# A fused two-layer decoder trunk: where a ones product stands in the DeltaNet projection, and when the output projections load their activations

## The reference, cut to what matters

```python
qkv = causal_dwconv_silu(qkv, conv_w)          # h @ w_in, a four-tap convolution per channel, SiLU
q, k, v = jnp.split(qkv, [A_QK, 2 * A_QK], axis=-1)
q = l2_norm(q.reshape(bsz, seq, A_HEADS, A_DK))  # x * rsqrt(sum(x*x over the 128 of a head) + eps)
k = l2_norm(k.reshape(bsz, seq, A_HEADS, A_DK))
...
return (o * jax.nn.silu(z)) @ w_out              # output projection of each mixer
x = x + gate * rms_norm(y, a_post_g[j])          # residual rows x are added behind it
```

## Time and profile before

| what | value |
|---|---|
| median of three runs | 3534.41 us |
| profiled execution, its own time | 3540.65 us |
| span of its records | 3539.0 us |
| PE busy | 3193.6 us (90%) |
| DVE, ACT, POOL busy | 1756.8, 1218.3, 940.8 us |
| mean granted TensorE clock | 0.949 of full speed |
| L892 square, L878 Ln, L880 Exp, one each | 1914, 1974, 1918 ns |
| L889, L878, L880 table load, one each | 1283 ns |
| L474 and L478 on POOL, mean of one | 3331 and 2586 ns |

### The profile page before, as it was taken

One profiled execution on the slowest core, in us unless ns is written; L12 is line 12 of the kernel. 1 busy time (PEld: TensorE's weight loads), 2 busy tenths in 40 slices (PEclk: granted clock), 3 DMA queues, 4 the chain that ended last, 5 costly groups with the idle time before them and its releaser, 6 DMA issues. The chain is left out here.

```text
span 3539.0 us, 41132 instructions
## 1 busy us (share of the span) xinstructions
PE 3193.6 (90%) x15158; PEld 2315.6 (65%) x15158; DVE 1756.8 (50%) x2771; ACT 1218.3 (34%) x2078; POOL 940.8 (27%) x739
## 2 busy tenths in 40 slices
PE   5889899999978997978999699996999999999798
PEld 4666566888867886866888578884444444444476
DVE  4454444566645665544211142115676777675433
ACT  4344445444414453224111131110344444444311
POOL 0578860233235440100000000001333333333210
PEclk8999899999989998988999899996999999999899
DMA  5233422567555654555431244317243433330333
GB/s 204 74 118 101 131 91 61 187 209 223 177 154 192 200 182 147 180 163 158 119 83 48 87 145 116 107 48 173 60 108 81 108 84 79 81 84 10 110 128 119
DMA packets 270102, 436.35 MB, mean 123 GB/s; under 512 B 73214, under 2 KB 170118, under 8 KB 259612
## 3 DMA queue, kind: packets, MB, share of 16 engines
q1 hardware_dynamic: 230812, 332.18, 31.8%
q0 software_dynamic: 23520, 86.21, 7.8%
q10 hardware_dynamic: 15600, 15.73, 1.5%
HBM read 283.10 MB, written 150.82 MB: 123 GB/s over the span
## 5 line engine op out<-in xcount | busy, mean ns | idle before, releaser
L2123 ACT ACTIVATE at_probs<-at_logits 128x512 f32<-128x512 f32 (+3 forms) x640 | 331.2, 532 | 414.0 <-PE at_logits L1986 381.7
L173 PE MATMUL pa_y<-pa_h_high,pa_w_high 128*128 128x512 f32 x1056 | 422.6, 400 | 7.5 <-ACT pa_acc L839 5.5
L1960 DVE TENSOR_REDUCE at_partial<-at_rough 128x1 f32<-128x512 f32 (+1 forms) x600 | 349.8, 605 | 129.1 <-PE at_rough L1948 76.3
L174 PE MATMUL pa_y<-pa_h_low,pa_w_high 128*128 128x512 f32 x1056 | 413.0, 391 | 0.0
L175 PE MATMUL pa_y<-pa_h_high,pa_w_low 128*128 128x512 f32 x1056 | 412.7, 391 | 0.0
L1873 POOL TENSOR_TENSOR at_sum_g<-at_sum_g,at_probs 128x512 f32<-128x512 f32 (+2 forms) x240 | 251.0, 1063 | 381.1 <-ACT at_probs L2123 380.0
L1997 PE MATMUL at_o<-at_probs,at_V 128*64 128x512 f32 (+3 forms) x1280 | 305.2, 555 | 2.9 <-ACT at_probs L2123 2.9
L1948 PE MATMUL at_rough<-at_K,at_Q 66*128 66x512 f32 (+1 forms) x600 | 250.1, 423 | 30.4 <-DMA at_K<-s_Fp 22.4
L1983 PE MATMUL at_logits<-at_Q,at_K 67*128 67x512 f32 (+3 forms) x640 | 260.9, 408 | 13.4 <-DMA at_Q<-at_minus_top 8.4
L1986 PE MATMUL at_logits<-at_Q,at_K 128*128 128x512 f32 (+3 forms) x640 | 254.0, 397 | 0.0
L173 PE MATMUL pk_y<-pk_h_high,pk_w_high 128*128 128x512 f32 x544 | 218.4, 401 | 30.4 <-POOL pk_ident L98 27.9
(11 more groups left out here) (348 smaller groups left out, 5685.8 us busy)
## 6 DMA issues: line engine op xcount, KB each, us to landing
at_Q<-s_Q SPq DMA_DIRECT2D x96, 256.0 KB, 6.8
s_qkv<-pa_sil POOLq DMA_DIRECT2D x16, 1024.0 KB, 6.6
pa_sil<-s_qkv SPq DMA_DIRECT2D x16, 1024.0 KB, 6.3
dr_kv<-s_qkv SPq DMA_DIRECT2D x16, 1024.0 KB
s_K<-pk_parts SPq DMA_DIRECT2D x32, 512.0 KB, 8.0
s_Q<-pb_parts SPq DMA_DIRECT2D x32, 512.0 KB, 8.0
at_K<-s_K SPq DMA_DIRECT2D x32, 512.0 KB, 5.7
pa_wraw<-in_a_w_in_dram ACTq DMA_DIRECT2D x15, 1024.0 KB
```

What stands on the lines that cost most here:

```text
L173: nc.tensor.matmul(out, w_high[:, k], h_high[:, k], start=k == 0, stop=False)
L174: nc.tensor.matmul(out, w_high[:, k], h_low[:, k], start=False, stop=False)
L1960: reduced.done(nc.vector.tensor_reduce(partial[:, h, qb * NQ + sub, grp:grp + 1], rough_bank(j, alone)[:, 0:width], AX.X, ALU.max))
L2123: probs_ok.done(nc.scalar.activation(probs[:, j % 3, h, off:BLK], logits[:, h, off:BLK], ACT.Exp))
```

## The change

Two edits. In stage `pa`, PE's ones product for tile T-1, its wait for the copied modulation row, and ACT's Ln and Exp move from behind block n = 2 of tile T to behind block n = 3 (`NB - 1`). In `output_projection`, POOL's loads of `u` and `xt` are separated: `u` of group c+2 is loaded once `u` of group c has been split (`u_split`), `xt` of group c+2 still once group c's output is complete. At the start both `u` loads stand ahead of both `xt` loads.

```diff
-                    if n == 2 and mod_summed_at(T) is not None:
+                    if n == NB - 1 and mod_summed_at(T) is not None:
                         pe.wait_ge(mod_copied, mod_summed_at(T) + 1)
-                    if n == 2 and 1 <= T <= QK:
+                    if n == NB - 1 and 1 <= T <= QK:
                         squared.wait(pe, T - 1)
                         for m in range(NB):
                             ins = nc.tensor.matmul(norm[:, m], ones[:, :], sq[:, m * BLK:(m + 1) * BLK], start=True, stop=True)
...
-                    if n == 2 and 1 <= T <= QK:
+                    if n == NB - 1 and 1 <= T <= QK:
                         summed.wait(act, T - 1)
...
-            def load(c, s):
+            def load_u(c, s):
                 pool.dma_start(u[:, s], s_uT.rearrange("(k p) t -> p k t", p=P)[:, :, bass.ds(c * P, P)]).then_inc(u_in[s], 16)
+
+            def load_x(c, s):
                 pool.dma_start(xt[:, s], x[bass.ds(c * P, P), :]).then_inc(x_in[s], 16)
 
             for s in range(2):
-                load(s, s)
+                load_u(s, s)
+            for s in range(2):
+                load_x(s, s)
...
                 for s in range(2):
+                    u_split.wait(pool, i * 2 + s, 0)
+                    load_u(i * 2 + (s + 2), s)
                     out_ok.wait(pool, i * 2 + s, 0)
-                    load(i * 2 + (s + 2), s)
+                    load_x(i * 2 + (s + 2), s)
```

## The result

The changed kernel takes 3480.95 us (median of four runs, 3479.71 to 3482.08), the kernel before 3535.23 us beside it: ratio 0.9846, 95% interval 0.9829 to 0.9863. The forecast was 3483 us, in a range of 3457 to 3508. The profiled execution took 3479.71 us (span 3478.1, mean granted clock 0.954).

A forecast was written before the change was run, and what follows sets the result against it. PE, 90% busy, was taken as the bound, with gains only from its waits. -35.0 us (projection) and -16.4 us (output projections) make -51.4 from the 3534.4 us median: 3483 us, range 3457 to 3508.

The forecast's parts named there:

- Five odd tiles: DeltaNet projection, odd tiles T = 3 to 11: wait before the ones product 4.4 us in place of 8.7, -21.7 us.
- First tiles: DeltaNet projection: first wait 7.5 us leaves 2.0 (-5.4); the second product's 3.7 becomes 1.5 (-2.1).
- Gates: End of the projection: new PE wait of 4.3 us for tile 15's first bank, 2 us slow clock behind it, +6.3 us.
- Slow clock: Projection: the ones product behind each odd tile's shorter wait takes 5.5 us and not 6.7, -5.5 us taken.
- Part 1: DeltaNet projection, ones product, Ln and Exp one block later: PE waits less for ACT's square, -35.0 us in sum.
- Part 2: Both output projections, activations' loads freed from the output: PE's waits for DVE's split go, -16.4 us together.
- Start order: Start of both output projections, group 1's u load second in POOL's queue: 1.4 us each, -2.8 us.
- (a): Projection, PE-bound: square in time in the five pairs as POOL and DVE mesh better; 3453 us, chance 0.13.
- (c): Projection, strict exclusion of DVE and POOL: square ends 44.3, not 40.9 us after the memset; +17, 3500 us, chance 0.12.
- (b): Projection: the square slips by nearly the block, waits stay at 8.7 us; +27, 3510 us, chance 0.13.
- (d): Projection: POOL falls behind in both tiles of a pair, slower than before; +8, 3542 us, chance 0.04.
- (e): Output projections: u lands no earlier for its split, so the loads' edit gains nothing; 3497 us, chance 0.04.

## Why the prediction was right

- **Five odd tiles.** Wait 4.4 forecast; measured 5.11, 4.72, 4.85, 5.28 and 4.55, mean 4.9. The memset to square distance was taken as 41.0 and was 40.8 to 41.8. The pairs take 60.1 us in the mean, forecast 59 to 60 (before: 64.4, where I had 65). The phase read in the first pair of before does hold for all. The size came out smaller: the step was to carry 27 of the 51 us, and gave 22. The five waits fell from 43.8 to 24.5 us (-19.3, forecast -21.7) and the five products behind them from 32.1 to 29.6 us (-2.6, forecast -5.5), because I had taken 6.7 us for each before, where they took 5.75 to 6.76, and 5.5 after, where they took 5.2 to 6.6. The table load is still released by the store, as forecast; I had named the store, and by the rows of the odd tile it is the smaller part (2.6 us, against 4.3 on DVE).
- **First tiles.** First wait forecast 2.0, measured 3.01: one us short. My 7.5 us for it before was also short, because the stretch in the earlier trace rows ends at 143.5 us and the wait lasted until 143.82; it was 7.8. Second forecast 1.5, measured 1.57. Last product: no wait, as forecast.
- **Gates.** Forecast a wait of 4.3 for the bank and 2 us of slow clock; 4.82 measured (1.0 before), with 0.63 us matmuls behind it, so the wait grew by 3.8. At the change to the v tiles PE doesn't wait (forecast +0.8): its next wait is at 838.5 us. Moving the gates took 6.6 us off the span.
- **Slow clock.** The product behind the wait of 5.11 us took 6.25, where I gave it 5.5 with its handover. The waits before the ones product are 29.1 in all, where the steps add up to 5 x 4.4 + 2.0 + 1.5 = 25.5.
- **Part 1 in all:** -35.0 forecast, -36.4 in the trace, -34 in the run of the edit alone. That the sum is so near is in part luck. The 5 us that the odd tiles fell short came back where I had counted nothing: the second product took 3.70 in place of 5.40 us, the first 5.40 in place of 6.04, a wait for the modulation row's copy shrank from 0.7 to 0.2, the waits behind 640 us from 5.5 to 4.5. And the trace of before is a long one: the same code ends the projection at 1015.5 us there and at 1011.2 in the trace of the second edit alone, against 979.0 to 980.0 in four traces with the changed projection. That makes 31 to 36 us.
- **Part 2.** Loop of ob forecast -12.4, its waits; -14.3 in the trace, 2 us more. The slow clock is not the reason, as the granted clock was full through the loop of before (row below: length, PE, PEld, DVE, ACT, POOL, granted clock, DMA). The rest is the restart: a wait is counted from the end of the matmul before it, and a matmul of 0.39 us is otherwise followed by the next after 0.23, so 0.16 us more are lost at each wait, and 0.11 behind it, where the first matmul is followed after 0.34 us. As an estimate that is 8 x 0.27 = 2.2 us. Start order forecast 2.8 us: in both stages together 3.5 in the trace, no difference that the runs can tell. In all -16.4 forecast, -17.5 in its run.

```profile
3344.00:3530.00 186.00, 173.55 (x756) 140.83 (x754) 69.39 (x63) 28.66 (x64) 20.14 (x28) 1.00 0.38 125
```

- **The rest.** The time fell by 54.3 us where the steps add to 51.4. The dr stage, whose code is unchanged, was 5.5 us shorter in the profiled execution; it lay between 285.0 and 292.4 us in all of the traces. With the product behind the third block it took 290.1 to 292.4 us (three traces), in the four traces with the changed kernel's projection 285.0 to 287.5, but 289.9 to 290.7 where that projection was faster still. So some 3 to 6 us of the gain may come with the first edit; by what way stays open, and no step of the forecast has it.
- **Rivals.** (a), the square in time, was possible but not by better meshing: it took the additions away. (c), strict exclusion, was priced as an addition to the wait, but it was already in the phase that I had copied from the rows of before. The Trainium skill (SBUF — State Buffer, Who interferes with whom) says that such a DVE and such a POOL operation exclude each other; for two-input operations on both sides the runs bear it out (14.12 against 7.12 us), for POOL's operation with one tensor input in part (9.34, while its own operation stretched from 2.85 to 5.01). That the second one blocks is not what the rows of the multiplication show: in the earlier trace rows it started first, and it was the one that stretched. I had read one 2.28 us scale beside a multiplication as evidence against the rule. It was a row of the other kind. (b), (d) and (e) did not happen: the waits shrank, no even tile waits, and the u loads come in time.
- **Not forecast:** in even tiles DVE's split now waits for the weights' DMA (up to 10.6 us), harmless, as scale waits for the Exp behind it anyway.

## What to carry to other kernels

Before moving a step to absorb a wait, ask what makes the awaited work long: here the first edit won 34 us by waiting later, and behind both edits 43 more were to be had by giving GpSimd's two-input operations to VectorE, which did both halves of a term in 1.3 us where GpSimd took 2.85 + 2.35. Write down the ring through the moved step: on the kernel before, where I put 2.7 us into the ring, the same move of work won 21 us in place of 43. How much of the difference is the 2.7 us was not run by itself. And read an elementwise operation's contention from rows of the same operand kinds.

## What the runs showed of the hardware

- DVE's scalar_tensor_tensor of 128 x 2048 takes 2.38 us alone and 4.7 beside back to back POOL additions of 128 x 1024, which themselves go from 2.35 to 3.9 us (the kernel without multiplications).
- It is not only operations with two tensor inputs that are held up. DVE's product with the first tap (L634) reads one tensor and takes 1.28 us alone; in the changed kernel it took 2.14 beside a multiplication, and 3.42 where a POOL addition had started 0.45 us before it. It ended 1.1 us after the addition:

```profile
183.38 2.78 POOL L478 TENSOR_TENSOR pa_PT<-pa_PT,pa_gb 128x1024 f32<-128x1024 f32 x1
183.83 3.42 DVE L634 TENSOR_SCALAR pa_acc<-pa_ybuf,pa_taps 128x2048 f32<-128x2048 f32 x1
```

- POOL's work is not free for being on an idle engine: 48 additions of 2.35 us, none on PE's path, cost 39 us of time (the changed kernel against the one without them).
- The granted clock was 0.50, the lower level (1.2 GHz), for the 3.6 us behind the wait of 4.82 us, with 0.63 us in place of 0.39 for a matmul of 512 columns; and 0.59 while the ones product behind the wait of 5.11 us ran:

```profile
559.80:563.40 3.60, 3.58 (x9) 2.83 (x10) 1.61 (x2) 3.57 (x5) 0.00 (x0) 0.50 0.00 0
231.00:237.30 6.30, 6.29 (x9) 2.75 (x10) 2.37 (x1) 3.19 (x6) 6.22 (x4) 0.59 0.68 231
```
